# The distance bias of attention: one VectorE operation a head, or two on GpSimd

## The chip, the cores and the metric

The kernel runs on one core of a Trainium2 chip. A core has TensorE (PE; its weight loads are shown apart as PEld), VectorE (DVE), ScalarE (ACT), GpSimd (POOL) and the queues of SyncE (SP) that issue transfers. Each engine works through its own instructions in order and waits on semaphores that the others count up. The metric is the device time of one execution in microseconds; lower is better.

## What is computed

Two layers over 256 positions of width 1024. Layer 0 is attention, layer 1 a diagonal state-space mixer, and each is followed by a gated convolutional feed-forward part. The change is in attention. Its reference, cut to what matters:

```python
score = ...                                   # indexer, one score per query and key
score = jnp.where(admissible[None], score, -jnp.inf)
_, idx = lax.top_k(score, n_keep)             # 64 keys per query
...
s_att = einsum(q, kg) * HEAD_DIM ** -0.5      # 16 heads of 64
dist = jnp.abs(tb[None, :, None] - idx)
s_att = s_att - slopes[None, :, None, None] * dist[:, None]
s_att = jnp.where(valid[:, None], s_att, -jnp.inf)
p = jax.nn.softmax(s_att, axis=-1)
out = einsum(p, vg) @ w_out
```

The kernel does not gather keys. It computes all scores of the 256 queries (384 columns on 128 partitions: 256 for the later queries, 128 for the earlier) and adds to them, per head, `slope * (-distance) + mask`, where the mask is 0 for a chosen key and -1e30 for the others. That sum is the bias, `bm`.

## The kernel before

Attention works on eight pairs of heads, p = 0 to 7, each with one of two buffers, a = p mod 2. The steps of a pair, with the engine and the lines:

- stage(p), GpSimd, L1504 to L1513: three copies of 128x256 bring q, k and v of the pair into `stage`. Pairs 0 and 1 are copied during the projection, the others in a loop, each after scores(p-2) (`s_done`).
- scores(p), TensorE, L504 to L516: the score products of two heads into PSUM (L510, L512) and the transposes of v (L515). It needs stage(p).
- masked(p), VectorE, L1251 to L1265: per head the bias (L1254, ndist times slope plus msk), then after scores(p) the scaled score plus bias (L1261, into `sp`, counted by `sp_ready`), then two maxima (L1264, L1265).
- exps(p), ScalarE, L866 to L872.
- normed(p), VectorE, L1272 to L1280: a reciprocal and four scalings of `sp` in place (L1277, L1279).
- turn(p), TensorE, L518 to L524: six transposes (L523). It needs normed(p).
- turned_out(p), ScalarE, L874 to L880: copies out the transposes (L877) and, after values(p), the result (L879); values(p), TensorE, L526 to L536; out_low(p), VectorE, L1282 to L1286 (L1284), after L879.

The order on each engine is written out by hand. VectorE runs masked(p+1), out_low(p-1), normed(p), v_out(p+1), and so on; TensorE runs scores(p+2), turn(p), values(p), and between these as filler the vector products `gemv` (L358 to L384) for the modulation of later stages: eight chunks, numbered 6 to 13, one a pair, each of four slots of 512 KB. SyncE loads chunk c+2 into the slots that chunk c has freed (L307 to L315). TensorE's whole list around the first pairs is: scores(0), scores(1), gemv(6), gemv(7), scores(2), turn(0), columns, values(0), gemv(8), scores(3), turn(1), half of gemv(9), values(1), the other half, scores(4), turn(2), and so on (L538 to L573). The last pairs have parts of the output projection as filler (L565, L568).

In the buffers, `bm`, `msk`, `ndist`, `sp` and `stage` all lie in the arena, so the trace calls them `arena`; the lines tell them apart. After attention GpSimd loads and computes constants of the state-space layer (L1558 to L1579), with its first arithmetic in L1545.

Of the kernel before, what the change touches and what calls it, by code (L numbers as in the profile page):

```python
# [25 lines left out]
ALU = mybir.AluOpType  # L26
# [8 lines left out]
PAIRS = HEADS // 2  # L35
# [46 lines left out]
def build(nc, t):  # L82
    with ExitStack() as ctx:
        def sb(name, shape, dt=F32):
            return ctx.enter_context(nc.sbuf_tensor(name, shape, dt))

        def sem(name):
            return ctx.enter_context(nc.semaphore(name))
# [30 lines left out]
        slope = sb("slope", [P, HEADS])  # L119
# [6 lines left out]
        def carve(cursor, n):  # L126
            a = arena[:, cursor[0]:cursor[0] + n]
            cursor[0] += n
            return a
# [7 lines left out]
        msk = carve(cur, 384)  # L137
        bm = carve(cur, 4 * 384).rearrange("p (a e t) -> p a e t", a=2, e=2)
# [8 lines left out]
        ndist = carve(cur, 384)  # L147
# [41 lines left out]
        def pr(name):  # L189
            return prm[:, PRM.index(name), :]  # L190
# [13 lines left out]
        small_in = sem("small_in")  # L204
# [22 lines left out]
        qkv_ready = sem("qkv_ready")  # L227
        idx_done, idx_relu, idx_acc = sem("idx_done"), sem("idx_relu"), sem("idx_acc")
        wit_ready = sem("wit_ready")
        sel = sem("sel")  # L230
        stage_ready, s_done, v_ready, bias_ready, sp_ready, mx_ready = (
            sem("stage_ready"), sem("s_done"), sem("v_ready"), sem("bias_ready"), sem("sp_ready"), sem("mx_ready"))
        exp_done, ri_ready, p_ready, tr_done, tr_out, pv_done = (
# [17 lines left out]
        N_PRM, N_ONES, N_EARLY, N_SMALL = 2, 4, 2, 4  # L251
# [784 lines left out]
        def _(dve):  # L1036
# [213 lines left out]
            dve.wait_ge(small_in, 16 * N_SMALL)  # L1250
            def masked(p, a):  # L1251

                for e in range(2):
                    dve.scalar_tensor_tensor(bm[:, a, e, :], ndist, slope[:, ds(2 * p + e, 1)], msk,  # L1254
                                             ALU.mult, ALU.add).then_inc(bias_ready, 1)
                dve.wait_ge(s_done, p + 1)
                if not (isinstance(p, int) and p < 2):
                    dve.wait_ge(tr_done, p - 1)
                for e in range(2):
                    dve.wait_ge(bias_ready, 2 * p + e + 1)  # L1260
                    dve.scalar_tensor_tensor(sp[:, a, e, :], acc[:, 2 * a + e, 0:384], HD ** -0.5, bm[:, a, e, :],  # L1261
                                             ALU.mult, ALU.add).then_inc(sp_ready, 1)
                dve.wait_ge(sp_ready, 2 * p + 2)
                dve.tensor_reduce(nmx[:, a, 0:2], sp[:, a, :, 0:T], AX.X, ALU.max, negate=True).then_inc(mx_ready, 1)  # L1264
                dve.tensor_reduce(nmx[:, a, 2:4], sp[:, a, :, T:T + P], AX.X, ALU.max, negate=True).then_inc(mx_ready, 1)  # L1265
# [16 lines left out]
            def out_low(p):  # L1282
# [3 lines left out]
                                  ALU.subtract).then_inc(act_lo, 1)  # L1286

            masked(0, 0)
            v_out(0, 0)
            masked(1, 1)  # L1290
            normed(0, 0)
            v_out(1, 1)
            split_lo(N_IN + SPL - 1)
            masked(2, 0)
            out_low(0)
            normed(1, 1)
# [204 lines left out]
        @block.gpsimd  # L1501
        def _(pool):

            for j, s in enumerate((S_Q, S_K, S_V)):  # L1504
                for a in range(2):
                    pool.wait_ge(qkv_ready, s + a + 1)
                    pool.tensor_copy(stage[:, a, j, :], qkv[:, s + a, :]).then_inc(stage_ready, 1)
            pool.wait_ge(qkv_ready, N_IN)
            with pool.Fori(1, PAIRS // 2) as i:
                for a in range(2):  # L1510
                    pool.wait_ge(s_done, 2 * i + a - 1)
                    for j, s in enumerate((S_Q, S_K, S_V)):
                        pool.tensor_copy(stage[:, a, j, :], qkv_f[:, ds((s + a + 2 * i) * T, T)]).then_inc(stage_ready, 1)  # L1513


            cnt = [0]

            def step(ins):

                ins.then_inc(pw, 1)  # L1520
                cnt[0] += 1
                pool.wait_ge(pw, cnt[0])

            def wide(name):
                return pr(name).unsqueeze(2).broadcast_to([P, PR, 32])

            def w3(a):
                return a.rearrange("p (n c) -> p n c", c=32)

            def b_at(k):  # L1530
                return bpow[:, :, :, LCH - 1 - k, :]

            def c_at(k):
                return cpow[:, k].rearrange("p r (n c) -> p r n c", c=32)

            def pace():

                if cnt[0] >= PW_FREE:
                    pool.wait_ge(a_lo, min(FT - 2, 1 + (cnt[0] - PW_FREE) // PW_STEP))

            def times(dst, src, re, im, minus_im):

                ops = (ALU.subtract, ALU.add) if not minus_im else (ALU.add, ALU.subtract)
                pace()
                step(pool.tensor_tensor(w3(t1), src[:, 0], wide(re), ALU.mult))  # L1545
                pace()
                step(pool.tensor_tensor(w3(t2), src[:, 1], wide(im), ALU.mult))
                pace()
                step(pool.tensor_tensor(dst[:, 0], w3(t1), w3(t2), ops[0]))
                pace()  # L1550
                step(pool.tensor_tensor(w3(t1), src[:, 1], wide(re), ALU.mult))
                pace()
                step(pool.tensor_tensor(w3(t2), src[:, 0], wide(im), ALU.mult))
                pace()
                step(pool.tensor_tensor(dst[:, 1], w3(t1), w3(t2), ops[1]))


            pool.wait_ge(act_lo, 16)  # L1558
            for ri_, name in ((0, "b_re"), (1, "b_im")):
                pool.dma_start(cpow[:, 1, ri_, :], t[name]).then_inc(ssm_in, 16)  # L1560
            for ri_, name in ((0, "c_re"), (1, "c_im")):
                pool.dma_start(cpow[:, 0, ri_, :], t[name]).then_inc(ssm_in, 16)
            pool.wait_ge(prm_v, PRM_STEPS)
            pool.wait_ge(ssm_in, 16 * N_SSM)
            times(b_at(0), c_at(1), "cre", "cim", False)
            for k in range(3):
                times(b_at(k + 1), b_at(k), "are", "aim", False)
            pace()
            step(pool.tensor_scalar(cpow[:, 0, 1, :], cpow[:, 0, 1, :], -1.0, None, ALU.mult))
            for k in range(3):  # L1570
                times(c_at(k + 1), c_at(k), "are", "aim", True)
            assert cnt[0] == PW_K

            pool.wait_ge(mod_used, 2 * CH * MS)
            pool.memset(mraw[:].rearrange("p a b -> p (a b)"), 0.0).then_inc(kz, 1)
            pool.wait_ge(k_done, 1)
            times(c_at(0), c_at(3), "are", "aim", True)
            assert cnt[0] == PW_ALL
            step(pool.memset(hst[:, :, :, 0:1], 0.0))  # L1579

            pool.wait_ge(tab_ready, 1)
            for mt in range(KT):
                pool.wait_ge(g2_ready, 8 * (mt + 1))
                pairs = slice(4 * mt, 4 * mt + 4)
                sh4 = [P, 2, 4, NJ]
                pool.tensor_tensor(rot1, g2, tcos_v[:, pairs, :].unsqueeze(1).broadcast_to(sh4), ALU.mult).then_inc(rot_s, 1)
                pool.tensor_tensor(rot2, g2, tsin_v[:, pairs, :].unsqueeze(1).broadcast_to(sh4), ALU.mult).then_inc(rot_s, 1)
                pool.wait_ge(rot_s, 2 * mt + 2)
                if mt:
                    pool.wait_ge(y_done, mt)  # L1590
                pool.tensor_tensor(hst[:, 0, :, 1:NJ], rot1[:, 0, :, 0:NJ - 1], rot2[:, 1, :, 0:NJ - 1],
                                   ALU.subtract).then_inc(h_ready, 1)
                pool.tensor_tensor(hst[:, 1, :, 1:NJ], rot1[:, 1, :, 0:NJ - 1], rot2[:, 0, :, 0:NJ - 1],
                                   ALU.add).then_inc(h_ready, 1)
                pool.wait_ge(h_ready, 2 * mt + 2)
# [110 lines left out]
```

## Time and profile before

| | |
|---|---|
| median of three runs | 802.56 us (801.44 to 803.48) |
| the profiled execution, its own time | 801.77 us |
| its span, first to last instruction | 800.0 us |
| PE busy | 742.9 us, 93% of the span |
| DVE busy | 584.6 us, 73% |
| ACT busy | 389.0 us, 49% |
| POOL busy | 175.4 us, 22% |
| mean granted TensorE clock | 0.969 |

The span is the time from the first to the last instruction of the profiled execution; the device time has 1.8 us more around it. A busy share is an average over stages with different limits, so the stage of the change is read by itself. In the rows below, times are microseconds from the start of the span; a timeline row gives the start, the duration, engine, line and operation, and in brackets the idle time before it and what ended it.

### The profile page before, as it was taken

What the parts mean: (1) busy time and instruction counts of PE and PEld (TensorE: products, weight loads), DVE (VectorE), ACT (ScalarE), POOL (GpSimd) and SP (SyncE); (2) the same over time, 40 slices, a digit from 0 to 9 for tenths busy, and PEclk for the clock granted to TensorE, in tenths of its full rate; (3) what the DMA queues carried; (4) which work ended last, traced back from release to release, by engine and by line L of the source; (5) the groups of instructions that cost most, each with busy time, mean ns of one, the idle gap of its engine ahead of it and who ended that gap; (6) DMA issues with size and microseconds to landing.
All of it is one profiled execution on the core that took longest, in us unless ns stands there. A gap on an engine that the chain in (4) does not pass through costs nothing.

```text
span 800.0 us, 17708 instructions
## 1 busy us (share of the span) xinstructions
PE 742.9 (93%) x6676; PEld 675.5 (84%) x6676; DVE 584.6 (73%) x948; ACT 389.0 (49%) x656; POOL 175.4 (22%) x115
## 2 busy tenths in 40 slices
PE   5778999999899999999999798989989999999996
PEld 1667999559798889898989688988979999999994
DVE  5666555984778888888998875686657667666675
ACT  4255445555464445444445442324456555555554
POOL 0000000301336444544444515542000000000000
PEclk9889999999899999999999889999999999999998
DMA  9898554896346776767775211112634555555531
GB/s 330 340 350 343 194 182 135 327 401 251 127 168 241 258 258 247 270 242 255 246 259 171 93 53 55 54 56 78 195 124 146 196 174 193 174 178 194 168 100 53
DMA packets 46842, 157.51 MB, mean 197 GB/s; under 512 B 6352, under 2 KB 7888, under 8 KB 46800
## 3 DMA queue, kind: packets, MB, share of 16 engines
q1 hardware_dynamic: 44064, 148.46, 53.3%
q10 hardware_dynamic: 2160, 6.38, 2.0%
q0 software_dynamic: 576, 2.10, 0.7%
q8 instruction: 28, 0.46, 0.2%
q14 instruction: 14, 0.11, 0.0%
HBM read 155.87 MB, written 1.05 MB: 196 GB/s over the span
## 4 chain that ended last, share of the span: by engine, by line
PE 62%; DVE 18%; issue 9%; ACT 6%; DMA 2%; SPq 1%; POOL 1%; DVEq 1%; ACTq 0%; POOLq 0%
PE up L345 10%; PE up L347 10%; PE up L346 10%; DVE wlo L1039 8%; PE acc L345 7%; PE acc L346 6%; PE acc L347 6%; ACT whi L749 3%; DVE ffn L1341 3%; PE gv L381 3%; DVE hl L1068 1%; DMA ffn<-in_mw 1%; DMA arena<-in_mw 1%; PE up L697 1%; PE acc L672 1%
## 5 line engine op out<-in xcount | busy, mean ns | idle before, releaser
L1039 DVE TENSOR_TENSOR wlo<-raw,whi 128x1024 fp32r<-128x1024 f32 x188 | 297.2, 1597 | 93.9 <-ACT whi L749 86.6
L345 PE MATMUL up<-hh,whi 128*128 128x256 f32 x896 | 257.3, 287 | 1.3 <-DVE hl L1068 0.8
L346 PE MATMUL up<-hl,whi 128*128 128x256 f32 x896 | 255.3, 285 | 0.0
L347 PE MATMUL up<-hh,wlo 128*128 128x256 f32 x896 | 255.2, 285 | 0.0
L749 ACT ACTIVATE whi<-raw 128x1024 fp32r<-128x1024 f32 x185 | 191.7, 1051 | 35.7 <-PE acc L347 24.4
L345 PEld LDWEIGHTS up<-hh,whi 128*128 128x128 f32 x896 | 173.8, 194 | 11.5 <-issue 9.9
L346 PEld LDWEIGHTS up<-hl,whi 128*128 128x128 f32 x896 | 173.9, 194 | 0.0
L347 PEld LDWEIGHTS up<-hh,wlo 128*128 128x128 f32 x896 | 173.7, 194 | 0.0
L345 PE MATMUL acc<-ah,whi 128*128 128x256 f32 x352 | 100.4, 285 | 6.8 <-DVE wlo L1039 6.6
L346 PE MATMUL acc<-al,whi 128*128 128x256 f32 x352 | 99.6, 283 | 0.0
L347 PE MATMUL acc<-ah,wlo 128*128 128x256 f32 x352 | 99.5, 283 | 0.0
L1341 DVE SCALAR_TENSOR_TENSOR ffn<-up,conv,ffn 128x254 f32<-128x254 f32 (+1 forms) x176 | 72.5, 472 | 32.3 <-ACT ffn L914 32.3
L345 PE MATMUL acc<-hh,whi 128*128 128x256 f32 x256 | 77.5, 303 | 9.6 <-DVE hl L1068 6.0
L914 ACT ACTIVATE ffn<-up,conv 128x256 f32<-128x256 f32 x88 | 44.9, 560 | 67.4 <-PE up L347 67.3
L346 PE MATMUL acc<-hl,whi 128*128 128x256 f32 x256 | 74.9, 292 | 0.0
L347 PE MATMUL acc<-hh,wlo 128*128 128x256 f32 x256 | 74.7, 292 | 0.0
L345 PEld LDWEIGHTS acc<-ah,whi 128*128 128x128 f32 x352 | 67.5, 192 | 8.4 <-DVE wlo L1039 8.4
L346 PEld LDWEIGHTS acc<-al,whi 128*128 128x128 f32 x352 | 67.5, 192 | 0.0
L347 PEld LDWEIGHTS acc<-ah,wlo 128*128 128x128 f32 x352 | 67.5, 192 | 0.0
L345 PEld LDWEIGHTS acc<-hh,whi 128*128 128x128 f32 x256 | 51.4, 201 | 13.8 <-issue 7.4
L346 PEld LDWEIGHTS acc<-hl,whi 128*128 128x128 f32 x256 | 51.7, 202 | 0.0
L347 PEld LDWEIGHTS acc<-hh,wlo 128*128 128x128 f32 x256 | 51.6, 202 | 0.0
(215 smaller groups left out, 963.1 us busy)
## 6 DMA issues: line engine op xcount, KB each, us to landing
raw<-in_w SPq DMA_DIRECT2D x188, 512.0 KB, 3.4
mraw<-in_mw SPq DMA_DIRECT2D x60, 512.0 KB, 6.2
arena<-in_mw SPq DMA_DIRECT2D x12, 512.0 KB, 11.6
raw<-in_w SPq DMA_DIRECT2D x12, 256.0 KB, 11.4
tmp<-in_mw SPq DMA_DIRECT2D x6, 512.0 KB, 7.7
ffn<-in_mw SPq DMA_DIRECT2D x6, 512.0 KB, 8.6
tmp<-in_mw ACTq DMA_DIRECT2D x4, 512.0 KB, 7.1
ffn<-in_mw ACTq DMA_DIRECT2D x4, 512.0 KB, 9.1
```

Of the source, the lines that this page charges most:

```text
L345: pe.matmul(out, w_h, xh, start=first, stop=False, skip_group_check=skip)
L346: pe.matmul(out, w_h, xl, start=False, stop=False, skip_group_check=skip)
L347: return pe.matmul(out, w_l, xh, start=False, stop=last, skip_group_check=skip)
L381: mm = pe.matmul(gv[32 * j:32 * j + 2, :], cond[:, k, 1 - odd:3 - odd], src[:, kk * 512:kk * 512 + 512], start=(k < 4 and not odd), stop=( ...
L672: mm = pe.matmul(acc[:, 2 + mt % 2, (2 * q + r) * NJ:(2 * q + r + 1) * NJ], bpow_r[:, r, c:c + P], ust[:, mt % 2, q, :], start=True, stop= ...
L697: mm = pe.matmul(y[32 * q:32 * q + 32, :, l], cpow[:, (l + 1) % 4, r, pair * 32:pair * 32 + 32], hst[:, r, q, :], start=False, stop=(l == ...
L749: act.activation(whi[:, n % SPL, :], raw[:, n % RAW, :], ACT.Copy).then_inc(hi_ready, 1)
L914: act.activation(cb[:, par, e, :], up[:, par, e * T:(e + 1) * T], ACT.Identity, scale=conv[:, layer, 2, ds(s + e * FT, 1)], bias=conv[:, l ...
L1039: dve.tensor_tensor(wlo[:, n % SPL, :], raw[:, n % RAW, :], whi[:, n % SPL, :].bitcast(F32), ALU.subtract).then_inc(lo_ready, 1)
L1068: dve.scalar_tensor_tensor(hl[:, k, :], tmp[:, k, :], modc[:, sh + k:sh + k + 1], hh[:, k, :].bitcast(F32), ALU.add, ALU.subtract).then_in ...
L1341: dve.scalar_tensor_tensor(cb[:, par, e, 1 + back:T], up[:, par, e * T:e * T + T - 1 - back], w, cb[:, par, e, 1 + back:T], ALU.mult, ALU. ...
```

## The change

VectorE no longer computes the bias. GpSimd does, in two operations a head: `tensor_scalar` multiplies ndist by the slope into `bm` (counted by a new semaphore `slant`), `tensor_tensor` adds msk in place (counted by `bias_ready`, on which L1260 waits as before). The biases of pairs 0 and 1 are computed when the mask is ready (`sel` at 35). For pair p from 2 on, GpSimd waits until VectorE has used the bias of pair p-2 (`sp_ready`), computes the bias of p, and only then waits for scores(p-2) and copies stage(p). The loop over the pairs is unrolled.

```diff
-        sel = sem("sel")
+        sel, slant = sem("sel"), sem("slant")
...
             def masked(p, a):
 
-                for e in range(2):
-                    dve.scalar_tensor_tensor(bm[:, a, e, :], ndist, slope[:, ds(2 * p + e, 1)], msk,
-                                             ALU.mult, ALU.add).then_inc(bias_ready, 1)
                 dve.wait_ge(s_done, p + 1)
...
+            def bias(p, a):
+
+                for e in range(2):
+                    pool.tensor_scalar(bm[:, a, e, :], ndist, slope[:, 2 * p + e:2 * p + e + 1], None, ALU.mult).then_inc(slant, 1)
+                for e in range(2):
+                    pool.wait_ge(slant, 2 * p + e + 1)
+                    pool.tensor_tensor(bm[:, a, e, :], bm[:, a, e, :], msk, ALU.add).then_inc(bias_ready, 1)
+
+            pool.wait_ge(small_in, 16 * N_SMALL)
+            pool.wait_ge(sel, 35)
+            for p in range(2):
+                bias(p, p)
             pool.wait_ge(qkv_ready, N_IN)
-            with pool.Fori(1, PAIRS // 2) as i:
+            for i in range(1, PAIRS // 2):
                 for a in range(2):
+                    pool.wait_ge(sp_ready, 4 * i + 2 * a - 2)
+                    bias(2 * i + a, a)
                     pool.wait_ge(s_done, 2 * i + a - 1)
                     for j, s in enumerate((S_Q, S_K, S_V)):
                         pool.tensor_copy(stage[:, a, j, :], qkv_f[:, ds((s + a + 2 * i) * T, T)]).then_inc(stage_ready, 1)
```

## Rows read from the trace of the kernel before

**Rows 1.** Busy time by stretch: PE, PEld, DVE, ACT, POOL; clock, DMA share, GB/s

```profile
137.70:189.90 52.20, 48.94 (x425) 31.10 (x426) 41.32 (x111) 29.40 (x89) 8.17 (x19) 1.00 0.80 312
151.40:157.39 5.99, 5.99 (x48) 2.82 (x44) 5.31 (x17) 3.65 (x15) 1.87 (x3) 1.00 1.02 412
183.20:189.90 6.70, 6.70 (x59) 6.39 (x60) 2.10 (x9) 2.38 (x4) 0.04 (x1) 1.00 0.16 63
```

**Rows 2.** Waits inside attention: total us, times, longest; then three in order of time

```profile
PE up L523 <- DVE arena L1279: 1.2, 3, 0.8
PEld up L523 <- DVE arena L1279: 2.2, 2, 1.2
DVE hl L1284 <- ACT hh L879: 9.2, 7, 3.9
...
150.39 0.15 PEld L381 LDWEIGHTS gv<-mraw,cond 128*2 128x2 f32 x6 [0.30 <-DMA mraw<-in_mw]
153.88 0.09 PEld L381 LDWEIGHTS gv<-tmp,cond 128*2 128x2 f32 x4 [0.32 <-DMA tmp<-in_mw]
156.43 0.09 PEld L381 LDWEIGHTS gv<-ffn,cond 128*2 128x2 f32 x4 [0.43 <-DMA ffn<-in_mw]
```

**Rows 3.** TensorE in order of time: scores (L510), turns (L523)

```profile
144.31 0.71 PE L510 MATMUL acc<-arena 64*128 64x256 f32 x4
146.41 0.87 PE L523 MATMUL up<-ident,arena 128*128 128x128 f32 x6 [0.79 <-DVE arena L1279]
...
157.39 0.71 PE L510 MATMUL acc<-arena 64*128 64x256 f32 x4
...
158.53 0.82 PE L523 MATMUL up<-ident,arena 128*128 128x128 f32 x6
```

**Rows 4.** VectorE in order of time: masking of pair 0, scaling of pair 2

```profile
139.65 1.02 DVE L1261 SCALAR_TENSOR_TENSOR arena<-acc,arena 128x384 f32<-128x384 f32 x2 [0.66 <-PE acc L515]
...
156.69 0.42 DVE L1284 TENSOR_TENSOR hl<-up,hh 128x256 f32 x1 [0.58 <-ACT hh L879]
...
157.96 0.28 DVE L1279 TENSOR_SCALAR arena<-arena 128x128 f32<-128x128 f32 x1
```

**Rows 5.** The bias operation of VectorE in attention, grouped by line

```profile
L1254 DVE SCALAR_TENSOR_TENSOR arena<-arena,slope 128x384 f32<-128x384 f32 x16 | 9.4, 628 | 0.0
```

**Rows 6.** GpSimd's stage copies in order of time

```profile
121.00 0.41 POOL L1507 COPY arena<-arena 128x256 f32<-128x256 f32 x1 [2.48 <-ACT arena L862]
139.80 1.09 POOL L1513 COPY arena<-arena 128x256 f32 x3 [18.40 <-PE acc L515]
```

**Rows 7.** GpSimd arithmetic by line: ns min/median/max

```profile
L1591 POOL TENSOR_TENSOR arena<-arena x8: 720/723/799, 482.3 to 542.4; 128x252 f32<-128x252 f32 x8
L1586 POOL TENSOR_TENSOR arena<-tmp,arena x8: 1269/1292/1316, 478.8 to 539.6; 128x512 f32<-128x512 f32 x8
L1569 POOL TENSOR_SCALAR arena<-arena x1: 3629/3629/3629, 330.3 to 330.3; 128x1024 f32<-128x1024 f32 x1
```

**Rows 8.** GpSimd and VectorE side by side, at 245, 328 and 146 us

```profile
245.29 1.92 POOL L1547 TENSOR_TENSOR arena<-arena,prm 128x1024 f32<-128x1024 f32 x1 [2.55 <-DVE al L1350]
245.67 2.62 DVE L1039 TENSOR_TENSOR wlo<-raw,whi 128x1024 fp32r<-128x1024 f32 x1 [0.52 <-ACT whi L749]
L1039 DVE TENSOR_TENSOR wlo<-raw,whi x188: 1205/1226/3421, 51.6 to 782.6; 128x1024 fp32r<-128x1024 f32 x188
...
328.24 5.08 DVE L1039 TENSOR_TENSOR wlo<-raw,whi 128x1024 fp32r<-128x1024 f32 x2 [0.53 <-ACT whi L749]
...
145.80 0.48 POOL L1513 COPY arena<-arena 128x256 f32 x1 [3.69 <-PE acc L515]
145.93 0.42 DVE L1279 TENSOR_SCALAR arena<-arena 128x128 f32<-128x128 f32 x1
```

**Rows 9.** The first arithmetic line of GpSimd: what stands before it, its longest wait

```profile
L1545 POOLq MODIFY_POOL_CONFIG  x2: 59/59/59, 192.2 to 192.2; - x2
...
  DMA arena<-in_c_im: 8.3, 1
```

## The prediction

> **What bounds the kernel now.** The engine table gives PE 93% busy and DVE 73%, so the first guess is that relief for VectorE is worth little; the stage of the change has to be read by itself. The change touches attention alone, from the ready mask at 137.8 us to the last output of a pair at 189.9. By the busy times of that stretch [rows 1] TensorE is busy 48.94 of 52.20 us at full clock, VectorE 41.32, GpSimd 8.17, and in a middle stretch of one pair TensorE is busy 5.99 of 5.99 and the transfer engines are full (share 1.02). Behind attention TensorE is again busy throughout (6.70 of 6.70). So TensorE's own list sets the pace, and what matters is where it waits. The waits [rows 2] name VectorE's scaling L1279 as what TensorE waited for: 1.2 us in the matmul rows, 2.2 us in the weight-load rows, which partly tell of the same pauses. The largest single one in the matmul rows is the 0.79 us before turn(0) [rows 3]. Three further waits, 0.30, 0.32 and 0.43 us, are for the filler's weights [rows 2], all between scores(2) at 144.31 and scores(4) at 157.39 [rows 3].
>
> Now VectorE. In the middle pairs it idles before out_low for ScalarE's L879 (0.58 us for pair 1 [rows 4], 9.2 us in 7 waits [rows 2]), and only then come out_low and normed. So normed(p), and with it turn(p), starts when values(p-1) has been copied out, and time freed in masked only lengthens that idle time. About 0.3 us lie between the end of normed(2) at 157.96 + 0.28 = 158.24 [rows 4] and turn(2) at 158.53 [rows 3]: that is all the room normed has.
>
> **What is removed.** 16 operations L1254 of 0.628 us mean, 9.4 us of VectorE [rows 5]. What of it is on TensorE's path is bounded by TensorE's waits for VectorE: 2.2 us at most, and I take the 0.8 before turn(0). Those of pair 0 lie in front of a wait for TensorE (0.66 us before L1261 [rows 4]) and are worth nothing; the middle ones fall into the idle time before out_low.
>
> **What is added.** 32 operations on GpSimd, four a pair. The add has two inputs in SBUF; GpSimd's nearest rows are 128x252 at 0.72 and 128x512 at 1.29 us [rows 7], and between them 384 columns come to 0.72 + 132/260 x 0.57 = 1.01, some 0.97 from start to start. The product has one input. Its lower bound is the copy: three of 256 columns in 1.09 us [rows 6], 1.35 ns a column, so 0.52 and with the start 0.57. Its upper bound is the only scalar operation of GpSimd in the trace, 3.63 us for 1024 columns [rows 7], so 1.36. That one ran beside two L1039 of VectorE that took 5.08 us together from 328.24 on [rows 8], so part of it is waiting; I take 0.57 and keep 1.36. One pair's bias is then 2 x 0.57 + 2 x 0.97 = 3.1 us.
>
> **Where it lies on the path: the start.** GpSimd begins at 137.9, and in its list stand the biases of pairs 0, 1 and 2 before the copies of stage(2). Before, those copies ran at 139.80 with time to spare [rows 6]. Now they end at 137.9 + 3 x 3.1 + 1.1 = 148.3, and scores(2), which stood at 144.31 [rows 3], begins there: **+4.0 us**. Behind it in TensorE's list stand turn(0), values(0) and all else. On VectorE L1261 of pair 0 ends about 0.7 later than 140.67 [rows 4], pair 1 likewise, and both are hidden behind the later scores(2). With TensorE 4 us late the waits of rows 2 and 3 go: the weights of chunks 8 and 9 were asked for before scores(2), so 1.05 us vanishes, and with it the 0.79 before turn(0): **-1.85**.
>
> **The middle.** For pair p GpSimd now needs 3.1 + 1.1 = 4.2 us, under the 6.0 us that a pair takes on TensorE [rows 1], so after the start it keeps up and copies come in time. But it works while VectorE does normed, for bias(p+3) is released by L1261 of pair p+1, which stands right before normed(p) on VectorE. The trace shows what that costs. At 245.67 an L1039 of VectorE, whose median is 1.226, takes 2.62 beside an operation of GpSimd that began at 245.29 and ends at 247.21 [rows 8]: it ends 1.08 after that, so it ran only when the other was done. For the scalings of normed there is one case: L1279 is 0.28 alone [rows 4] and 0.42 beside a copy of 256 columns, which in turn is 0.48 in place of 0.41 [rows 6, 8]. With an add of 0.97 before it, a scaling waits about 0.8, with a copy about 0.2. Of the four scalings of a pair I count one behind an add and two behind copies or products, 1.2 to 1.5 us; the 0.3 of room off, 1.1 is left a pair. Four pairs, 1 to 4, do it beside the biases 4 to 7: **+4.4**. The Trainium skill speaks to this in "SBUF — State Buffer", section "Who interferes with whom": a VectorE operation of one input that runs in a two-port mode, and GpSimd, exclude each other for the whole instruction. By that rule the scalings wait in full, as in my sum; did only operations of two SBUF inputs collide, the sum would lose the 4.4. The trace agrees in its one case (0.42 against 0.28).
>
> **The tail.** Pairs 5 to 7 have no bias left beside them, so nothing is lost or won. Behind attention TensorE has no idle time in which the delay could go, and GpSimd's later work starts on the last out_low, so all moves along. The unrolled loop and the two new waits are some 0.05 us each on GpSimd, inside the 1.8 us a pair that it has free. The filler's transfers move with the slots that they wait for: a chunk of 4 x 512 KB takes 5.1 us at the 412 GB/s of rows 1, less than a pair takes before or after, so I count nothing for them.
>
> Sum: 4.0 - 1.85 + 4.4 = **+6.5 us**. The profiled execution took 801.77 with a span of 800.0; the median of the runs is 802.56, 0.8 above it, and the forecast is 802.56 + 6.5 = **809.1**.
>
> **The rivals.**
> - *The product on GpSimd is slow* (1.05 to 1.36). For it: L1569. Against: the copies, and the two L1039 beside it. Start + 6 x 0.48 = 2.9, and some 2 more in the middle: 814; at 1.36 a pair takes 5.8 us on GpSimd, nearly as much as on TensorE, and it comes to 817.
> - *The scalings do not collide with GpSimd.* For it: nothing but that there is one case only. Then 4.0 - 1.85 = +2.2: 804.7.
> - *No loss: GpSimd gets done in time.* This is the other side. It decides at the copies of stage(2): they must end by 144.31 + 1.85 = 146.2, so a bias may cost (146.2 - 137.9 - 1.1)/3 = 2.4 us in place of 3.1, and there must be no collisions. That needs products and adds below the ones in [rows 6, 7]: 802.5. Even with everything hidden the gain is at most the 2.2 us that TensorE waited for VectorE. "GPSIMD Engine Reference", section "Engine selection", of the Trainium skill has one-input operations at about line rate and two-input ones at half of VectorE's; by its figure of 4497 ns for 2048 columns an add would be an estimated 0.84, and the sum about 2 us less.
> - *Code for GpSimd has to be loaded on the path.* Before its first arithmetic a configuration instruction runs at 192.2, and the wait behind it, 8.3 us, ends with a transfer [rows 9], which hides what it may cost. Now it comes earlier. I expect it right behind the last copy at 121.00 [rows 6], 17 us before it is needed; if it stood behind the wait for the mask, up to 8.3 us would be added: 815 or so. "GPSIMD Engine Reference", section "Instruction dispatch", gives about 6 us for such a load; no row here shows it alone.
>
> **How the numbers follow.** Forecast 0.48, slow product 0.25, no collisions 0.11, no loss 0.09, code load 0.07. The range 804.3 to 816.5 leaves out the no-loss case and the far ends. A measurement tells 0.3% from no change, 2.4 us here. Of the case without collisions (+2.2) half counts as no change, so: slower 0.84, same 0.13, faster 0.03, for the bound of 2.2 us on the gain is itself below 2.4.
>
> **What would show it.** scores(2) at about 148.3 with the last stage copy of GpSimd as releaser, and turn(0) with no wait for VectorE; GpSimd's product 0.57 and add 1.0; L1277 and L1279 at up to 1.2 us in pairs 1 to 4 and 0.28 to 0.35 in pairs 5 to 7; turn(1) to turn(4) waiting for L1279; the configuration instruction near 121; attention ending near 196.5. Wrong would be: scores(2) at its old place, scalings at their old durations, or a product of 1 us and more.

## The result, and the profile after

The changed kernel takes 822.09 us (median of 4 runs, 820.42 to 822.59) against 803.02 for the kernel before in the same session (4 runs, 801.44 to 803.57): a ratio of 1.0237, with a 95% interval of 1.0216 to 1.0259. It is slower, as forecast, but by 19 us and not by 6.5, outside the range. The profiled execution has a span of 820.8 us (800.0 before).

From the page of the changed kernel, its engine line and the TensorE clock over 40 slices of 20.5 us:

```profile
PE 753.0 (92%) x6676; PEld 680.5 (83%) x6676; DVE 581.1 (71%) x932; ACT 388.8 (47%) x656; POOL 210.5 (26%) x147
...
PEclk9889999688989999999999959999998999999999
```

GpSimd has 35.1 us more to do and VectorE 3.5 less, although L1254 held 9.4 us of it [rows 5]. TensorE is busy 10.1 us longer with the same 6676 matmuls. That is the first sign: its work did not grow, it became slower. The eighth slice of the clock line (143.6 to 164.2 us, near the start of attention) has a 6; in the kernel before the granted clock is 1.00 there [rows 1].

**GpSimd.** Its timeline from the last early copy on (start, duration, operation, and in brackets the idle time before), and its operations by tile (minimum, median and maximum in ns):

```profile
120.65 0.40 POOL L1504 COPY arena<-arena 128x256 f32<-128x256 f32 x1 [2.48 <-ACT arena L862]
137.66 2.46 POOL L1508 TENSOR_SCALAR arena<-arena,slope 128x384 f32<-128x384 f32 x2 [16.60 <-DVE arena L1246]
140.10 1.95 POOL L1511 TENSOR_TENSOR arena<-arena 128x384 f32<-128x384 f32 x2
...
150.82 2.07 POOL L1524 COPY arena<-arena 128x256 f32<-128x256 f32 x3
...
160.70 1.96 POOL L1511 TENSOR_TENSOR arena<-arena 128x384 f32<-128x384 f32 x2
162.60 1.08 POOL L1524 COPY arena<-arena 128x256 f32<-128x256 f32 x3
```
```profile
L1508 POOL TENSOR_SCALAR arena<-arena,slope x16: 1232/1240/1259, 137.7 to 183.8; 128x384 f32<-128x384 f32 x16
L1511 POOL TENSOR_TENSOR arena<-arena x16: 980/994/1083, 140.1 to 186.0; 128x384 f32<-128x384 f32 x16
...
L1508 POOLq MODIFY_POOL_CONFIG  x2: 11/11/11, 121.0 to 121.0; - x2
```

The add takes what was forecast (0.99 against 1.0). The product takes 1.24 us where 0.57 was taken, in all 16 cases. A pair's bias costs 4.4 us and not 3.1. The copies of stage(2) end at 152.89; the first of the three started while VectorE was in an L1039 that ran from 150.26 to 151.95, and the three took 2.07 us where 1.07 to 1.20 is usual for the later pairs. The configuration instruction sits at 121.0, right behind the last early copy.

**TensorE.** Its scores (L510) and turns (L523) in order of time; of the kernel before, five rows that were not shown:

```profile
137.97 0.71 PE L510 MATMUL acc<-arena 64*128 64x256 f32 x4 [0.61 <-issue]
...
152.95 1.23 PE L510 MATMUL acc<-arena 64*128 64x256 f32 x4 [8.90 <-POOL arena L1524]
...
162.42 0.71 PE L510 MATMUL acc<-arena 64*128 64x256 f32 x4
...
164.61 0.87 PE L523 MATMUL up<-ident,arena 128*128 128x128 f32 x6 [0.89 <-DVE arena L1276]
168.43 0.71 PE L510 MATMUL acc<-arena 64*128 64x256 f32 x4
...
171.79 1.54 PE L523 MATMUL up<-ident,arena 128*128 128x128 f32 x6 [2.07 <-DVE arena L1276]
179.37 0.71 PE L510 MATMUL acc<-arena 64*128 64x256 f32 x4
...
184.27 0.71 PE L510 MATMUL acc<-arena 64*128 64x256 f32 x4
...
187.62 0.87 PE L523 MATMUL up<-ident,arena 128*128 128x128 f32 x6 [2.05 <-DVE arena L1276]
195.14 0.86 PE L510 MATMUL acc<-arena 64*128 64x256 f32 x4
```
```profile
138.31 0.71 PE L510 MATMUL acc<-arena 64*128 64x256 f32 x4 [0.61 <-issue]
...
163.15 0.71 PE L510 MATMUL acc<-arena 64*128 64x256 f32 x4
...
168.05 0.71 PE L510 MATMUL acc<-arena 64*128 64x256 f32 x4
169.53 0.87 PE L523 MATMUL up<-ident,arena 128*128 128x128 f32 x6 [0.19 <-DVE arena L1279]
174.21 0.71 PE L510 MATMUL acc<-arena 64*128 64x256 f32 x4
```

The same 1.23 and 0.71 us for four L510 is the second sign. The clock itself stands in the busy times by stretch (PE, PEld, DVE, ACT, POOL; clock, DMA share, GB/s), cut where TensorE stood still and started again:

```profile
143.90:152.90 9.00, 0.14 (x4) 0.00 (x0) 6.13 (x12) 4.03 (x17) 9.00 (x11) 0.71 0.97 380
152.90:162.40 9.50, 9.45 (x52) 6.57 (x52) 3.99 (x7) 2.94 (x10) 9.50 (x11) 0.55 0.11 44
162.40:171.80 9.40, 6.45 (x59) 3.59 (x55) 8.05 (x17) 3.42 (x11) 6.32 (x10) 0.99 0.88 315
171.80:179.40 7.60, 7.60 (x44) 4.99 (x44) 4.13 (x9) 3.02 (x10) 5.20 (x7) 0.56 0.41 165
179.40:187.60 8.20, 6.17 (x58) 3.56 (x54) 6.82 (x16) 3.42 (x11) 5.80 (x9) 1.00 0.84 310
187.60:195.10 7.50, 7.48 (x42) 4.06 (x42) 4.19 (x13) 2.94 (x10) 0.49 (x2) 0.57 0.61 234
```

Three times the granted clock is near 0.5, its lower level (1.2 of 2.4 GHz), and each of the three stretches of slow work begins where a wait of TensorE ends, or 1 us behind it: 8.90, 2.07 and, with the 1 us, 2.05. The clock had come down before the first wait ended (0.71 over it). In all it stood at the lower level for 27.3 us of attention, in three pieces of 13.7, 6.8 and 6.8 us. In the kernel before it is 1.00 through all of attention [rows 1]. "TensorE: Matmul & The Clock Gate" of the Trainium skill, section "Part 1: The HAM clock gate", has the clock set by how busy TensorE was shortly before, with these two levels; the rows agree.

**VectorE.** Scalings of pair 1 and pair 2 (L1274 of 256 columns, L1276 of 128), then of pair 5:

```profile
160.96 2.87 DVE L1274 TENSOR_SCALAR arena<-arena 128x256 f32<-128x256 f32 x1
...
169.30 1.01 DVE L1276 TENSOR_SCALAR arena<-arena 128x128 f32<-128x128 f32 x1
170.23 1.09 DVE L1274 TENSOR_SCALAR arena<-arena 128x256 f32<-128x256 f32 x1
...
192.91 0.35 DVE L1274 TENSOR_SCALAR arena<-arena 128x256 f32<-128x256 f32 x1
193.17 0.28 DVE L1276 TENSOR_SCALAR arena<-arena 128x128 f32<-128x128 f32 x1
```

In pair 5, with nothing beside them, they take 0.35 and 0.28; in pair 2, beside GpSimd, up to 1.09 and 1.01. The one at 160.96 ends at 163.83, and in the timeline of GpSimd above two adds and three copies stand from 160.70 to 163.68: it was held up until five operations in a row had passed.

**Where the 21.4 us are.** Attention, from the first row of scores(0) to that of turn(7), takes 206.44 - 137.97 = 68.5 us; before it took 185.35 - 138.31 = 47.0. Cut at the rows of L510 and L523:

| stretch | before | after | more | what is in it |
|---|---|---|---|---|
| scores(0) to scores(2) | 6.00 | 14.98 | +9.0 | late copies of stage(2) |
| scores(2) to scores(3) | 7.09 | 9.47 | +2.4 | half clock; the waits before turn(0) (0.79) and for chunk 8 (0.30) are gone |
| scores(3) to turn(1) | 1.27 | 2.19 | +0.9 | wait for scaling, 0.89 |
| turn(1) to scores(4) | 4.72 | 3.82 | -0.9 | DMA waits gone (0.32, 0.43) |
| scores(4) to turn(2) | 1.14 | 3.36 | +2.2 | wait for scaling, 2.07 |
| turn(2) to scores(5) | 4.62 | 7.58 | +3.0 | half clock |
| scores(5) to scores(6) | 4.90 | 4.90 | 0.0 | |
| scores(6) to turn(4) | 1.48 | 3.35 | +1.9 | wait for scaling, 2.05 (before 0.19) |
| turn(4) to scores(7) | 4.68 | 7.52 | +2.8 | half clock |
| scores(7) to turn(7) | 11.14 | 11.30 | +0.2 | |

So about 9.0 are the late start, 5.0 the waits for scalings, and the half clock has 3.0 + 2.8 + 0.2 and, in its first stretch, 2.4 plus the 1.1 of waits that it hides: 9.5. Some 2 are given back. The busy times tell the same without the table: over attention TensorE runs the same 384 matmuls in 53.34 us where it took 44.39, 9.0 more, and stands idle for 15.1 us instead of 2.7, 12.5 more. The span grew by 20.8; later stages return the last 0.6.

### The profile page after: what moved, and what is told of

It is laid out like the page before. It is cut to its first block, busy times and chain, and to the rows that moved or that the text cites. A ratio compares the mean times of both kernels' runs of the same rounds, so it can differ in the third digit from the quotient of the medians.

```text
span 820.8 us, 17692 instructions
## 1 busy us (share of the span) xinstructions
PE 753.0 (92%) x6676; PEld 680.5 (83%) x6676; DVE 581.1 (71%) x932; ACT 388.8 (47%) x656; POOL 210.5 (26%) x147
## 4 chain that ended last, share of the span: by engine, by line
PE 65%; DVE 15%; issue 8%; ACT 5%; POOL 2%; DMA 2%; SPq 1%; DVEq 0%; ACTq 0%; POOLq 0%
PE up L345 10%; PE up L347 10%; PE up L346 10%; PE acc L345 7%; PE acc L346 7%; PE acc L347 7%; DVE wlo L1039 6%; ACT whi L749 3%; PE gv L381 3%; DVE ffn L1338 2%; DVE hl L1068 1%; DMA ffn<-in_mw 1%; DMA arena<-in_mw 1%; PE misc L392 1%; PE up L523 1%
## 5 line engine op out<-in xcount | busy, mean ns | idle before, releaser
L1039 DVE TENSOR_TENSOR wlo<-raw,whi 128x1024 fp32r<-128x1024 f32 x188 | 293.0, 1575 | 96.5 <-ACT whi L749 88.9
```

The lines of the kernel that those rows point to most:

```text
L1039: dve.tensor_tensor(wlo[:, n % SPL, :], raw[:, n % RAW, :], whi[:, n % SPL, :].bitcast(F32), ALU.subtract).then_inc(lo_ready, 1)
```

## The experiments

The expectations name their theories by letter and say what each holds for their run. Theory A is the account of the table: a late start, scalings that GpSimd shuts out, and the half clock that TensorE's idle time in either place brings on. Its rivals leave one of these out: above all that the delay costs its own length and the clock has no part of its own (theory C), or that the steady load of GpSimd on every pair is the cost (theory B). The expectation of late_stage2 still splits the loss as 9.0, 11.3 and some 4 us; the table is the later reckoning. "Extra" below is the length of attention, scores(0) to turn(7), above the 47.0 us of the kernel before in its profile, read from the one profiled execution of each run; ratios are to the kernel before, run beside each.

**late_stage2: a late start alone.** In the kernel before, GpSimd fills a tile that nothing reads, 17 times, between the mask and its copies. VectorE keeps the bias.

```diff
+            pool.wait_ge(small_in, 16 * N_SMALL)
+            pool.wait_ge(sel, 35)
+            for n in range(17):
+                pool.memset(spare, 0.0).then_inc(spare_set, 1)
+                pool.wait_ge(spare_set, n + 1)
```

> The kernel before, with 17 memsets of 768 unused columns put on GpSimd between the ready mask and the copies of stage(2); the bias stays on VectorE. It holds scores(2) back as the change does and leaves the later pairs alone. Theory A (the change costs 9.0 us at the start because the copies stand behind three biases, then 11.3 us because TensorE falls to the half clock after idle times, then some 4 us because GpSimd and the scalings of normed exclude each other): scores(2) near 152, one stretch of about 8.6 us at half clock behind it, no more than that, 7.8 + 4.3 - 1.85 = 10 us over the kernel before. Theory B (the loss is the steady load of GpSimd on every pair, the start is absorbed later): at most 2 us over it. Theory C (position counts, the clock does not): 7.8 - 1.85 = 6 us over it.

Measured: 1.0129 [1.0100, 1.0159], extra 10.6. Two rows of TensorE and two stretches:

```profile
151.77 1.23 PE L511 MATMUL acc<-arena 64*128 64x256 f32 x4 [8.65 <-POOL arena L1519]
161.41 0.71 PE L511 MATMUL acc<-arena 64*128 64x256 f32 x4
```
```profile
151.70:161.40 9.70, 9.63 (x52) 6.61 (x52) 4.17 (x13) 2.94 (x10) 2.14 (x7) 0.55 0.18 71
161.40:195.20 33.80, 31.97 (x289) 20.82 (x286) 26.26 (x74) 17.46 (x55) 4.24 (x9) 1.00 0.93 358
```

The extra is what theory A gave (10) and neither B (at most 2) nor C (6). With none of the change in it, the late stage(2) alone brings the half clock (0.55) and 9.64 us from scores(2) to scores(3) (before 7.09). Behind it the clock stays at 1.00, since no scaling is late. So the start and its clock are about half of the loss; the other half needs the collisions.

**warm: the late start with TensorE kept busy.** In the changed kernel 70 matmuls whose result nobody reads stand ahead of scores(2).

```diff
+            def warm(n):
...
+                for _ in range(n):
+                    pe.matmul(misc[:, T:2 * T], whi[:, W_OUT % SPL, 0:P], hl[:, KT - 1, :], start=True, stop=True,
+                              skip_group_check=True)
...
+            warm(70)
```

> The changed kernel, with 70 matmuls of 256 columns into an unused part of PSUM between gemv(7) and scores(2), some 8.3 us that fill the idle time there. Theory A: the granted clock stays full through the first pairs, scores(2) stands where it stood in the changed kernel, and 4.3 us come back: a ratio to before of 1.018 in place of 1.024; the later two stretches at half clock stay. Theory C: nothing comes back, 1.024.

Measured: 1.0103 [1.0059, 1.0147], a spread of 809.4 to 817.5 over four runs; the profiled execution is the slowest of them, 817.54 us, extra 14.3.

```profile
146.04 8.65 PE L542 MATMUL misc<-hl,whi 128*128 128x256 f32 x70
...
182.56 0.87 PE L523 MATMUL up<-ident,arena 128*128 128x128 f32 x6 [2.06 <-DVE arena L1284]
```
```profile
140.00:155.10 15.10, 14.65 (x122) 11.07 (x122) 8.52 (x16) 6.58 (x20) 15.10 (x16) 1.00 0.66 250
155.10:168.00 12.90, 11.91 (x106) 7.32 (x106) 8.83 (x23) 6.36 (x21) 12.90 (x16) 1.00 0.57 209
168.00:182.60 14.60, 12.40 (x97) 7.13 (x97) 10.80 (x24) 6.44 (x21) 13.98 (x19) 0.88 0.85 322
182.60:190.10 7.50, 7.50 (x42) 4.05 (x42) 4.11 (x13) 2.94 (x10) 0.43 (x2) 0.56 0.55 210
```

scores(2) is as late as in the changed kernel (15.09 us after scores(0), against 14.98), and 7.1 us of attention are back all the same. Of these, 3.7 us lie between scores(2) and scores(3), now at full clock (5.76 us, against 9.47), and 1.3 between turn(2) and scores(5); the waits before turn(1) and turn(2) are shorter by 2.3 (none and 0.67, against 0.89 and 2.07). That these waits shrink too had not been expected, and what shortens them is not shown. The profiled execution lies near the expectation (817.54 over 804.09, the median of the kernel before beside it, is 1.017); the median of the runs is better. The half clock behind the 2.06 us wait is still there in this execution, and the second stretch is down to 3.4 us; 10.2 us of attention are at the half level in place of 27.3. The time goes with the clock from execution to execution too: 817.54 and 815.58 us have a mean granted clock of 0.962, 809.43 and 810.17 one of 0.972 and 0.970, which is 13 to 17 us less at the half level. Where in the program that was is not on record.

**one_port_after: the scalings in another form.** In the changed kernel each scaling also adds a zero that lies in PSUM, which keeps its value. One small matmul ahead of scores(0) writes the zeros.

```diff
-                    dve.tensor_scalar(sp[:, a, e, 0:T], sp[:, a, e, 0:T], ri[:, a, e:e + 1], None,
-                                      ALU.mult).then_inc(p_ready, 1)
...
+                    dve.scalar_tensor_tensor(sp[:, a, e, 0:T], sp[:, a, e, 0:T], ri[:, a, e:e + 1], misc[:, T:2 * T],
+                                             ALU.mult, ALU.add).then_inc(p_ready, 1)
...
```

> The changed kernel, with the four scalings of normed written as scale plus a zero from PSUM (scalar_tensor_tensor, one input from SBUF, the other from PSUM), so that they need only VectorE's own ports. Theory A: they take 0.3 to 0.45 us also beside GpSimd, TensorE's waits for them (5.2 us in four) fall to about 1.2, and without those waits the second and third stretch at half clock go too, 7 us: about 811 us, ratio 1.010; scores(2) stays 9 us late. Rival (only operations with two inputs in SBUF collide with GpSimd, and the scalings were late for another reason): 1.024 as before.

Measured: 1.0097 [1.0061, 1.0133], extra 11.4. The rows that decide: the group of the larger scalings, a turn, and two stretches from scores(2) and scores(3) on.

```profile
L1276 DVE SCALAR_TENSOR_TENSOR arena<-arena,misc 128x256 f32<-128x256 f32 x16 | 7.7, 478 | 0.3
```
```profile
168.72 0.87 PE L523 MATMUL up<-ident,arena 128*128 128x128 f32 x6 [0.58 <-DVE arena L1278]
```
```profile
151.90:161.90 10.00, 9.97 (x52) 6.62 (x52) 5.41 (x13) 2.95 (x10) 10.00 (x11) 0.52 0.25 100
161.90:197.30 35.40, 32.27 (x291) 20.89 (x287) 23.48 (x64) 17.43 (x55) 17.96 (x25) 1.00 0.89 342
```

By itself the form is slower, 0.478 against 0.35 us, but GpSimd no longer holds it up: between 160 and 200 us all are 0.475 to 0.482. TensorE's longest wait for one is 0.62 us, and the second and third stretch of half clock are gone. "SBUF — State Buffer" of the Trainium skill, section "Who interferes with whom", says that VectorE operations with at most one input in SBUF, outside the two-port modes, do not contend with GpSimd, and that a `tensor_scalar` can be in such a mode; the two forms behave as it says.

**one_port_before: the same form in the kernel before,** as a control.

> Control: the kernel before with the one-port scalings. They take about 0.42 and 0.29 us in place of 0.35 and 0.28, some 0.2 us a pair on VectorE: ratio 1.000 to 1.002. Were it 0.998 or less, the gain of the one-port form in the changed kernel would in part be its own.

Measured: 1.0012 [0.9994, 1.0031], extra 2.3; clock 0.97 over attention, with some 3.4 us at the half level from 147.9 on. The form brings nothing in a kernel whose bias is on VectorE, so its gain above is not its own; it costs attention some 2 us there.

**copies_first: GpSimd copies stage(p) before it computes the bias of p.**

```diff
-                    pool.wait_ge(sp_ready, 4 * i + 2 * a - 2)
-                    bias(2 * i + a, a)
                     pool.wait_ge(s_done, 2 * i + a - 1)
...
+                    pool.wait_ge(sp_ready, 4 * i + 2 * a - 2)
+                    bias(2 * i + a, a)
```

> The changed kernel, with the wait for scores(p-2) and the copies of stage(p) put ahead of bias(p). Biases 0 and 1 still stand before the copies of stage(2). Theory A: scores(2) near 147.6, 3.3 us late in place of 9, a short idle time after which the clock may hold: 5.5 + 4.3 us come back, about 812 us, ratio 1.012, and the collisions with normed stay. Theory B (steady load of GpSimd): 820 or more, since every operation is still there.

Measured: 1.0102 [1.0076, 1.0129], extra 10.9.

```profile
147.84 1.23 PE L510 MATMUL acc<-arena 64*128 64x256 f32 x4 [3.45 <-POOL arena L1522]
```
```profile
144.40:147.80 3.40, 0.00 (x0) 0.00 (x0) 1.53 (x3) 1.54 (x8) 3.40 (x7) 0.86 0.84 314
147.80:158.00 10.20, 9.85 (x52) 6.47 (x52) 8.62 (x18) 5.28 (x19) 10.20 (x11) 0.54 0.66 267
```

scores(2) starts 9.53 us after scores(0) where it was 14.98, and TensorE idles for 3.45 us, not 8.90. It falls to the half level all the same: a bias less at the start buys the delay back, not the clock. The start gives 5.5 of the 10.5 us of attention that come back. Behind it the waits for scalings are shorter too, 0.32, 1.09 and 0.88 us, and the last two are followed by only 3.4 us each at the half level; 17.1 us of attention are at it in place of 27.3. The steady load of GpSimd is the same as in the changed kernel, so theory B (820 or more) is out.

**two_input_product: the product as a `tensor_tensor`,** with the slope broadcast along the columns.

```diff
-                    pool.tensor_scalar(bm[:, a, e, :], ndist, slope[:, 2 * p + e:2 * p + e + 1], None, ALU.mult).then_inc(slant, 1)
+                    pool.tensor_tensor(bm[:, a, e, :], ndist, slope[:, 2 * p + e:2 * p + e + 1].broadcast_to([P, 384]), ALU.mult).then_inc(slant, 1)
```

> The changed kernel with the product written as tensor_tensor of ndist with the slope broadcast along the row, in place of tensor_scalar. The broadcast sums of GpSimd took 1.92 us for 1024 columns, so 384 should take 0.75 us, against 1.24 of the scalar form: a bias 3.4 us in place of 4.4, scores(2) near 149.6 in place of 152.95. Theory A: 3.3 us back at the start and a little behind it, ratio 1.018 to 1.020. Rival (the scalar form was slow because of the place, not of the form): 1.024 as before.

Measured: 1.0146 [1.0112, 1.0181], extra 12.7.

```profile
L1508 POOL TENSOR_TENSOR arena<-arena,slope x16: 819/826/1803, 137.5 to 176.7; 128x384 f32<-128x384 f32 x16
```

The same product takes 0.83 us with two inputs and 1.24 with one and a scalar. It gave more than expected. Every 0.4 us is paid six times before stage(2), and scores(2) starts 11.3 us after scores(0); the waits for scalings fall to 1.55 and 1.54 us; and 17 us are at the half level in place of 27.

**no_product: the add alone.** The slopes are left out of the computation; GpSimd adds the mask to the distances, one operation a head.

```diff
-                    pool.tensor_scalar(bm[:, a, e, :], ndist, slope[:, 2 * p + e:2 * p + e + 1], None, ALU.mult).then_inc(slant, 1)
-                for e in range(2):
-                    pool.wait_ge(slant, 2 * p + e + 1)
-                    pool.tensor_tensor(bm[:, a, e, :], bm[:, a, e, :], msk, ALU.add).then_inc(bias_ready, 1)
+                    pool.tensor_tensor(bm[:, a, e, :], ndist, msk, ALU.add).then_inc(bias_ready, 1)
```

> The changed kernel without the product with the slopes: GpSimd only adds ndist and msk (the slope is left out of the computation), two operations of 0.97 us a pair in place of four. Theory A: a bias costs 1.95 us, the copies of stage(2) end near 137.7 + 5.9 + 1.1 = 144.7 us, no idle time to speak of before scores(2), full clock; what is left is the exclusion with the scalings, 1 to 4 us: ratio 1.002 to 1.005. Theory B (any load of GpSimd on every pair costs the bulk): 1.012 or more.

Measured: 1.0011 [0.9985, 1.0037], extra 2.2.

```profile
137.17 5.83 POOL L1508 TENSOR_TENSOR arena<-arena 128x384 f32<-128x384 f32 x6 [16.56 <-DVE arena L1246]
142.94 1.10 POOL L1521 COPY arena<-arena 128x256 f32<-128x256 f32 x3
```
```profile
144.09 0.71 PE L510 MATMUL acc<-arena 64*128 64x256 f32 x4 [0.49 <-POOL arena L1521]
```

A bias of 1.95 us a pair is below the 2.4 that the forecast's other side set as its point of decision, and the kernel is then level with the one before. It does not beat it, though VectorE is free of L1254: TensorE waits 1.14 us before turn(0), 0.56 before turn(2) and 0.54 before turn(4).

**warm_one_port and repaired: both causes taken away.** warm_one_port has 64 matmuls ahead of scores(2) and the scalings with the zero; repaired has in addition the copies first, and 26 matmuls. Since the filler writes where the zero lies, a small matmul behind it writes the zeros, and VectorE's scalings of pair 0 wait for that one.

> The changed kernel with both: 64 filling matmuls in TensorE's idle time before scores(2), and scalings that need only VectorE's own ports. What is left is the late start alone. Theory A (start, half clock and exclusion are three separate costs that add up): full clock throughout attention, no TensorE wait for a scaling over 0.7 us, attention some 7 us longer than before, ratio 1.009. Rival (the two repairs give back the same microseconds): no better than the better of the two alone, 1.010, with attention 11 us longer.

> The changed kernel with the copies of stage(p) ahead of bias(p), one-port scalings and 26 filling matmuls before scores(2). Every known cost but the time of the biases themselves is gone. Theory A: scores(2) 3.3 us late, full clock, attention 2 to 4 us longer than before, ratio 1.004, that is no gain even so, since bias(1) on GpSimd is ready 3 us after VectorE had it. Rival (with its defects repaired the move pays, since VectorE is relieved of 9.4 us): at or under 1.000.

Measured: warm_one_port 1.0080 [1.0056, 1.0104], extra 8.2, clock 1.00 over attention. repaired 1.0069 [1.0045, 1.0092], extra 6.5, with 3.4 us at the half level. The first is as expected (1.009); the second is a miss (1.004 was expected): scores(2) is still 3.6 us late and TensorE waits 0.83 us before turn(0) and 0.55 to 0.62 us before turns 1, 2, 4 and 6.

```profile
138.70:194.50 55.80, 52.17 (x454) 34.97 (x455) 35.34 (x92) 27.05 (x85) 41.75 (x50) 1.00 0.77 292
```

With the changed kernel these make a square of four: extra 21.4 as it is, 14.3 with the filler, 11.4 with the other scalings, 8.2 with both. The filler is worth 7.1 alone and 3.2 beside the other form, the form 10.0 and 6.1: the two causes overlap, because each idle time of TensorE can bring the clock down. The square rests on one profiled execution of each, and that of warm is its slowest. By the medians of the runs the excess over the kernel before is 19.1 us as it is, 8.8 with the filler, 7.1 with the other scalings and 6.4 with both: the same order, and an overlap that is larger still. With the clock at 1.00 the late start is left: scores(2) is 8.1 us late, the extra is 8.2. No repair gets below the kernel before, though the repaired ones also carry what the slower form costs (2.3 us of attention in one_port_before).

**pair1_only: the one bias that VectorE's critical stretch could spare.** In the kernel before, GpSimd computes the bias of pair 1 alone, ahead of its copies.

```diff
-                for e in range(2):
+                if not (isinstance(p, int) and p == 1):
+                    for e in range(2):
...
+            for e in range(2):
+                pool.tensor_scalar(bm[:, 1, e, :], ndist, slope[:, 2 + e:3 + e], None, ALU.mult).then_inc(slant, 1)
+            for e in range(2):
+                pool.wait_ge(slant, e + 1)
+                pool.tensor_tensor(bm[:, 1, e, :], bm[:, 1, e, :], msk, ALU.add).then_inc(bias1, 1)
```

> The kernel before with the bias of pair 1 alone on GpSimd, ahead of its copies of stage(2) and stage(3): 4.4 us from the mask, ready at 142.1, where VectorE would reach it at 142.0. It saves VectorE the 1.14 us between masked(0) and masked(1). Theory A: the 0.79 us before turn(0) goes, and the waits of the filler for its weights, which end at fixed times in the next 10 us, take it back: 0.998 to 1.001, nothing that can be measured. Rival (VectorE's relief is worth what it frees): 0.9985 or less.

Measured: 1.0000 [0.9974, 1.0027]; attention is 0.6 us shorter, and turn(0) waits for VectorE no more. That is what was to be had by freeing VectorE here, and it is below what the runs can tell.

## Why the prediction was wrong in size and right in direction

- **The start, +4.0.** It was +9.0. The place and the mechanism were right: TensorE waited for the last stage copy behind three biases. What failed is the price of the product, taken at its lower bound from the copy [rows 6] at 0.57; its upper bound from L1569 [rows 7] was nearly the truth: 1.36 there, 1.24 measured. That both have one input did not make the copy the nearest row; the operation of the same kind was. Three pairs at 2.5 us in products instead of 1.1 make 4 of the missing 5, and the copies that ran beside VectorE's L1039 make 1.0. On VectorE the masking of pair 0 ended 2.0 us later and not 0.7, hidden as stated. The rival of the slow product had the price but carried it through to 814 to 817 only.
- **The rule that favoured the change.** "GPSIMD Engine Reference", section "Engine selection", of the Trainium skill puts one-input operations at about line rate and two-input ones below. The runs show otherwise for this pair: 1.24 us for the product with a scalar, 0.99 for the add, 0.83 for the product with a broadcast input. The estimate of 0.84 for the add, from the page's figure, met 0.99.
- **The middle, +4.4.** The waits for scalings came to 0.89, 2.07 and 2.05 = 5.0 us. The term was about right and unevenly spread: four even shares of 1.1 were forecast, and one pair (3) had none. That is not the clock's doing: turn(3) waits for a scaling in none of the twelve profiles, at full clock (before, warm_one_port) no more than at half. A scaling stopped behind five operations of GpSimd (2.87 us) was not foreseen; "one behind an add and two behind copies or products" assumed that VectorE gets its turn after each.
- **The waits that go, -1.85.** The wait before turn(0) and the DMA waits went, as stated: about 2 in the table.
- **The step that is missing** is the clock. The sum priced each idle time of TensorE at its own length. The profile of before says 1.00 for attention [rows 1], and the text never asked what keeps it there. Some 9 us of the 21.4 (9.0 by the busy times, 9.5 by the table) are TensorE's own work at the half level, behind idle times that the forecast had itself put into TensorE's list (4.0 us at once, then 1.1 a pair). late_stage2 and warm show it from both sides.
- **The tail, the configuration instruction, the DMA queues** cost nothing, as stated: pairs 5 to 7 have scalings of 0.35 and 0.28 and no half clock of their own; the instruction stood at 121.0.
- **The gain.** Nothing contradicts that freeing VectorE is worth 2.2 us at most: pair1_only takes 0.6 us off attention, no_product none.

What stays open is the exact condition under which the clock falls. one_port_before, repaired and no_product each have some 3.4 us at the half level behind waits of 0.8 to 1.1 us, and warm has as much behind one of 0.67; the kernel before has a wait of 0.79 and the changed kernel one of 0.89 with no fall behind them.

## What to carry to other kernels

An idle time of the engine that sets the pace costs its own length and, on TensorE, the work behind it at half clock: here waits of 2 us cost 3 more each. So look at the granted clock by stretch before and after, and price a delay of TensorE twice. Take the price of an added operation from the row of the same kind on the same engine, however odd that row looks, and before moving work to GpSimd ask what stands behind it in its list and which of VectorE's operations it shuts out.

## What was not expected of the hardware

- The granted clock fell while TensorE idled for 8.90, 3.45 and 2.07 us, and 1 us after the end of a wait of 2.05. Then it stayed at the half level for 7 to 9 us of work, although TensorE was busy throughout (7.60 of 7.60 us at 0.56). Waits of 1.54 and 1.09 us (two_input_product, copies_first) were each followed by 3.4 us at it.
- GpSimd multiplies 384 columns by a scalar in 1.24 us but by a broadcast input in 0.83; 16 operations each, with medians within 0.02 of their minima. Its add of two inputs takes 0.99.
- A scaling of VectorE, 0.35 us by itself, stood for 2.87 us while five operations of GpSimd passed. With an addend in PSUM it took 0.478 us whatever GpSimd did.
